# Two-layer audio trunk on one core: the tokens around the inner norms in two halves, squares summed on TensorE

## The reference

```
for layer in range(DEPTH):
    h = rms_norm(x, norm_mix_pre[layer])
    if layer % 2 == 0:
        m = even_mixer(h, w_in, ..., w_out)      # RG-LRU branch and stick-breaking attention
    else:
        m = odd_mixer(h, positions, w_qkv, sinks, w_o)   # sliding-window attention with rotary
    x = x + rms_norm(m, norm_mix_post[layer])
    h = rms_norm(x, norm_ffn_pre[layer])
    f = conv_ffn(h, w_up, conv_w, conv_b, w_down)        # D_FF = 2816, gated, width-3 conv
    x = x + rms_norm(f, norm_ffn_post[layer])
```

## Time and profile before

| | |
|---|---|
| time, median of 3 runs | 1190.69 us (1187.4 to 1191.2) |
| the profiled execution: its own time | 1188.73 us |
| its span | 1186.9 us |
| PE busy | 1149.5 us (97% of the span), 5888 matmuls |
| DVE busy | 692.9 us (58%) |
| ACT busy | 486.1 us (41%) |
| POOL busy | 73.2 us (6%) |
| TensorE clock granted, mean | 0.993 |

### The profile page before, as it was taken

The page is one execution under the profiler, slowest core; times in us unless marked ns, Lnnn a source line. Parts: engine busy times, 40 slices in busy tenths (PEclk is TensorE's granted clock), DMA queues, the critical chain, the costliest instruction groups (busy, mean ns, idle before and its releaser), DMA issues.

```text
span 1186.9 us, 14989 instructions
## 1 busy us (share of the span) xinstructions
PE 1149.5 (97%) x5888; PEld 959.4 (81%) x5888; DVE 692.9 (58%) x840; ACT 486.1 (41%) x667; POOL 73.2 (6%) x57
## 2 busy tenths in 40 slices
PE   8999999999999999999999998899999999999997
PEld 6875777777888888888887788786888888899997
DVE  5745455558876766732228677248877766752222
ACT  4555655434533443431123229334444443433220
POOL 3000000122000000000112100033000000000000
PEclk9999999999999999999999999999999999999999
DMA  6312112222333332322321541041423333332221
GB/s 212 107 36 72 36 36 71 71 72 71 107 84 93 106 104 77 103 98 98 98 98 36 156 129 49 1 126 34 135 79 105 106 88 88 106 98 65 96 99 71
DMA packets 147477, 104.39 MB, mean 88 GB/s; under 512 B 4642, under 2 KB 144354, under 8 KB 147426
## 3 DMA queue, kind: packets, MB, share of 16 engines
q1 hardware_dynamic: 146466, 102.36, 29.0%
q10 hardware_dynamic: 960, 1.31, 0.5%
HBM read 98.02 MB, written 2.10 MB: 84 GB/s over the span
## 4 chain that ended last, share of the span: by engine, by line
PE 84%; DVE 7%; ACT 6%; issue 1%; POOL 0%; DMA 0%; POOLq 0%; SPq 0%; DVEq 0%; ACTq 0%
PE ps L1283 25%; PE ps L1285 25%; PE ps L1284 25%; DVE x L1076 3%; PE ps L1480 2%; PE ps L1468 2%; ACT hx_hi L656 1%; DVE hx_lo L1080 1%; ACT prob L772 1%; PE ps L1491 1%; PE ps L1352 1%; ACT w_hi L522 1%; PE ps L1345 1%; PE ps L1504 1%; PE ps L1660 1%
## 5 line engine op out<-in xcount | busy, mean ns | idle before, releaser
L1283 PE MATMUL ps<-hx_hi,w_hi 128*128 128x512 f32 x912 | 360.5, 395 | 2.7 <-DVE hx_lo L1080 2.5
L1284 PE MATMUL ps<-hx_lo,w_hi 128*128 128x512 f32 x912 | 355.9, 390 | 0.0
L1285 PE MATMUL ps<-hx_hi,w_lo 128*128 128x512 f32 x912 | 355.7, 390 | 0.0
L810 DVE TENSOR_TENSOR w_lo<-w_raw,w_hi 128x2048 fp32r<-128x2048 f32 (+1 forms) x90 | 201.9, 2243 | 169.5 <-ACT w_hi L522 169.4
L522 ACT ACTIVATE w_hi<-w_raw 128x2048 fp32r<-128x2048 f32 (+1 forms) x90 | 168.4, 1871 | 159.2 <-DMA w_raw<-in_ffn_w_down 113.8
L1283 PEld LDWEIGHTS ps<-hx_hi,w_hi 128*128 128x128 f32 x912 | 171.5, 188 | 45.8 <-DVE hx_lo L1080 7.2
L1285 PEld LDWEIGHTS ps<-hx_hi,w_lo 128*128 128x128 f32 x912 | 171.6, 188 | 36.3
L1284 PEld LDWEIGHTS ps<-hx_lo,w_hi 128*128 128x128 f32 x912 | 171.7, 188 | 35.2 <-issue 0.7
L1283 PE MATMUL ps<-w_hi,g_hi 128*128 128x256 f32 x352 | 99.2, 282 | 0.0
L1285 PE MATMUL ps<-w_hi,g_lo 128*128 128x256 f32 x352 | 98.9, 281 | 0.0
L1284 PE MATMUL ps<-w_lo,g_hi 128*128 128x256 f32 x352 | 98.9, 281 | 0.0
(11 more groups left out here) (202 smaller groups left out, 1524.1 us busy)
## 6 DMA issues: line engine op xcount, KB each, us to landing
w_raw<-in_ffn_w_up SPq DMA_DIRECT2D x88, 512.0 KB, 5.0
w_raw<-in_ffn_w_down SPq DMA_DIRECT2D x16, 1024.0 KB, 5.1
w_raw<-in_even_w_in SPq DMA_DIRECT2D x8, 1024.0 KB, 5.1
w_raw<-in_ffn_w_down SPq DMA_DIRECT2D x8, 768.0 KB, 4.4
w_raw<-in_odd_w_qkv SPq DMA_DIRECT2D x6, 1024.0 KB, 5.0
w_raw<-in_even_w_out SPq DMA_DIRECT2D x4, 1024.0 KB, 5.1
w_raw<-in_odd_w_o SPq DMA_DIRECT2D x4, 1024.0 KB, 5.7
x_in<-in_x SPq DMA_DIRECT2D x4, 512.0 KB, 6.4
```

The lines of the kernel that those rows point to most:

```text
L810: dve.tensor_tensor(w_lo[s][:, 0:k], w_raw[s][:, 0:k], w_hi[s][:, 0:k], ALU.subtract).then_inc(w_lo_done, 1)
L1283: pe.matmul(dst, s_hi, r_hi, start=first, stop=False)
L1284: pe.matmul(dst, s_hi, r_lo, start=False, stop=False)
L1285: return pe.matmul(dst, s_lo, r_hi, start=False, stop=last)
```

## The change

- **Halves.** At each boundary the last units of the first product (units 1, 2 and 3 of an output projection; the last three of the down projection) are computed for tokens 0 to 255 first, all of them, and then for tokens 256 to 511. The first two units of the next product are done the same way. A matmul there has 256 columns instead of 512, and there are twice as many. The two output tiles of a half share a bank.
- **The first norm** is done per half: `post_mean_square` and `post_spread` for half 0 stand inside half 1 of the first product, those for half 1 inside half 0 of the next product. POOL still adds most squares of m; the last square buffer goes into PE's sum directly (6 one-column matmuls per half).
- **The second norm's squares** aren't added on POOL: PE multiplies each of the eight squared tiles with the column of ones (`mean_square(p, i)`, 4 one-column matmuls each), and there are three buffers `sq`, freed by PE.
- `keep_clock` is no longer called at the boundaries.
- **Copies** of m out of PSUM for the halved units are made by ACT; DVE keeps m·g·r in PSUM (columns 256 to 511 of bank 6 or 7) instead of in `m`.
- **Extra slots.** The first unit of each up projection has a weight slot of its own. Its load needs no ring slot, only that the attention of its layer is over.
- **Small moves.** `split_at` splits unit u+4 at the first unit of an up projection and nothing at the second and third. Layer 0's unit 2 of the output projection is no longer used as filling before `ya_ready`. `sw_values` (layer 1's attention) takes its eight products in the order 0, 4, 1, 5, 2, 6, 3, 7; the first four write partitions 0 to 63, the others 64 to 127.

```diff
 def split_at(layer, u):
-    return {0: u + 3, 1: u + 3, 2: None}.get(u - U_UP[layer], u + 2)
+    return {0: u + 4, 1: None, 2: None}.get(u - U_UP[layer], u + 2)
...
 # ACT
-    for i in range(DT):
-        act.wait_ge(x_new, DT * bi + i + 1)
-        act.activation(hx_hi[:, i, :], x[:, i, :], ACT.Identity, scale=gain(which, layer, i)).then_inc(hx_hi_done, 1)
-        square(n + 1, i, x[:, i, :])
-    split_hi(u + 2)
-    root(n + 1)
+    act.preload_act_table_set("sqrt_and_others")
+    for j, v in enumerate(last):
+        half_out(bi, 0, j, v)          # square, and copy to m
+    post_root(bi, 0)
+    if bi != 1:
+        half_out(bi, 1, 0, last[0])
+    for i in range(DT):
+        hi(0, i)
+        if i == (4 if bi == 1 else 3):
+            split_hi(splits[0])
+        if i == 5 and bi != 1:
+            half_out(bi, 1, 1, last[1])
+    half_out(bi, 1, len(last) - 1, last[-1])
+    split_hi(splits[1])
+    post_root(bi, 1)
+    for i in range(DT):
+        hi(1, i)
+        square(bi + 1, i, x[:, i, :])  # from i = 3 on: waits for PE's sum of square i - 3
+        if i == (3 if bi == 1 else 5):
+            split_hi(splits[2])
+    root(bi + 1)
...
 # PE
-def mean_square(n):
-    ...
+def mean_square(p, i):
+    if i == 0:
+        pe.wait_ge(pstd_done, 2 * p)
+    pe.wait_ge(sq_done, DT * p + i + 1)
+    for t in range(TT):
+        last = pe.matmul(bank(6)[:, t:t + 1], sq[i % 3][:, P * t:P * t + P], ones[:, 0:1], start=i == 0 and t == 0,
+                         stop=i == DT - 1 and t == TT - 1, skip_group_check=True)
+    last.then_inc(xms_mm, 1)
...
-    mean_square(n)
-    keep_clock(7, 6)
-    spread(n)
-    keep_clock(13, 7)
-    first_two(u, ...)
-    spread(n + 1)
+def first_units(bi, u):
+    pe.wait_ge(ahalf_evac, a_copied)
+    for j in range(2):
+        unit_ready(u + j)
+        for k in range(UK):
+            if j == 0 and k == 3:
+                post_mean_square(bi, 1)
+            if j == 0 and k == 6:
+                post_spread(bi, 1)
+            pe.wait_ge(hx_ready, DT + 2 * DT * bi + k + 1)
+            first_half(u + j, 0, k)
+    pe.wait_ge(group_evac, evac)
+    for k in range(UK):
+        pe.wait_ge(hx_ready, 2 * DT + 2 * DT * bi + k + 1)
+        for j in range(2):
+            last = first_half(u + j, 1, k)
+            ...
+        if k >= 2:
+            mean_square(bi + 1, k - 2)
+    unit(u + 2, hx, hooks={(0, 0): lambda: mean_square(bi + 1, DT - 2), (0, 1): lambda: mean_square(bi + 1, DT - 1),
+                           (0, 5): lambda: spread(bi + 1)})
...
+ # out_halves(layer), h = 0 then 1, units 1 to 3, 8 tiles each:
+                    for k in ks[j]:
+                        if h and step == 3:
+                            ...
+                            post_mean_square(bi, 0)
+                        if h and step == 5:
+                            post_spread(bi, 0)
...
-            for e in range(8):
+            for e in (0, 4, 1, 5, 2, 6, 3, 7):
```

More of the change, by code:

```diff
@@ L54 @@
 G_SHIFT = N_DOWN - 4
[L57 to L63, removed]
+HALF = T // 2
+N_BOUNDARY = 3
 V_CONV = 64
@@ L375, in load_cols @@
             slot_free(u)
-            load(u, cols(w, c0), whole(u % RING))
+            load(u, cols(w, c0), whole(slot(u)))
         w_in, w_qkv = io["even_w_in"][0], io["odd_w_qkv"][0]
@@ L461, in load_up @@
                 for b in range(2):
-                    load(u, cols(w_up, j * P + F * b, P), w_raw[u % RING][:, :, b, :])
-            for j in range(2):
+                    load(u, cols(w_up, j * P + F * b, P), w_raw[slot(u)][:, :, b, :])
+            if layer == 0:
+                sp_.wait_ge(av_mm, SB_HEADS)
+            else:
+                sp_.wait_ge(o_mm, NCH)
+            for j in range(4):
                 load_up(U_UP[layer] + j, j)
@@ new lines, in boundary, with hi @@
+        def boundary(bi, which, layer, last, splits):
+            def hi(h, i):
+                act.wait_ge(x_new, 2 * DT * bi + DT * h + i + 1)
+                act.activation(hx_hi[:, i, tokens_of(h)], x[:, i, tokens_of(h)], ACT.Identity,
+                               scale=gain(which, layer, i)).then_inc(hx_hi_done, 1)
+            act.preload_act_table_set("sqrt_and_others")
[19 more added lines that the diff above has]
+            root(bi + 1)
@@ L1516, in out_part, with out_half, down_half, first_half @@
                 last.then_inc(unit_done, 1)
+        def out_half(layer, j, h, k, first, last):
+            u = U_OUT[layer] + j
+            hi, lo = mixer_out(layer, k)
+            for b in range(2):
+                dst = bank(group_banks(group_of(u)) + h)[:, tokens_of(b)]
+                ins = three(dst, *weights(u, k, b), hi[:, tokens_of(h)], lo[:, tokens_of(h)], first and b == 0, last and b == 1)
+            return ins
+        def down_half(u, h, k, k0):
+            for b in range(2):
+                dst = bank(group_banks(group_of(u)) + h)[:, tokens_of(b)]
+                ins = three(dst, *weights(u, k - k0, b), g_hi[:, k, tokens_of(h)], g_lo[:, k, tokens_of(h)],
+                            k == 0 and b == 0, k == FT - 1 and b == 1)
+            return ins
+        def first_half(u, h, k):
+            for b in range(2):
+                dst = bank(group_banks(group_of(u)) + h)[:, tokens_of(b)]
+                ins = three(dst, *weights(u, k, b), hx_hi[:, k, tokens_of(h)], hx_lo[:, k, tokens_of(h)], k == 0 and b == 0,
+                            k == UK - 1 and b == 1)
+            return ins
         pe.wait_ge(consts_cast, 1)
@@ L1552, in _ @@
[L1552 to L1570 removed]
+        out_whole(0, [7], end=True)
@@ L1572, in ffn @@
+        def out_projection(layer):
+            if layer == 1:
+                pe.wait_ge(y_ready, NCH)
+                banks_free(group_of(U_OUT[1]))
+                unit_ready(U_OUT[1])
+                out_whole(1, range(UK), first=True, end=True)
+            out_halves(layer)
         def ffn(layer, bi):
             u0 = U_UP[layer]
-            n = 4 * layer + 1
-            boundary(n, bi, u0)
-            for j in range(2, 5):
+            first_units(bi, u0)
+            for j in range(3, 5):
@@ L1583, in ffn @@
             g_up = group_of(U_DOWN[layer])
-            for mp in range(4):
+            for mp in range(3 + layer):
                 b0 = group_banks(g_up + mp)
@@ L1618, in _ @@
         ffn(0, 0)
-        boundary(3, 1, U_QKV)
-        for k in range(2, N_QKV):
+        down_halves()
+        first_units(1, U_QKV)
+        for k in range(3, N_QKV):
             u = U_QKV + k
```

507 lines of the change are left out of this document (322 added, 185 removed).

## The result

| | before | after |
|---|---|---|
| median (range) | 1190.95 us (1187.4 to 1191.22, 4 executions) | 1206.89 us (1198.41 to 1210.45, 4 executions) |
| profiled execution, span | 1188.73, 1186.9 us | 1210.45, 1208.7 us |
| mean granted clock over the span | 0.993 | 0.975 |
| PE busy, matmuls | 1149.5 us, 5888 | 1172.8 us, 6734 |

The ratio is 1.0131, 95% interval [1.0074, 1.0187]: the kernel became 16 us slower. 1194.5 was forecast. The profiled execution of after is the slowest of its four (1210.45 us, mean clock 0.975); the fastest took 1198.41 us at 0.987.

What follows compares the result with a forecast made beforehand. PE's stream was taken as the bound: boundary work -1.8, waits +8.3 and attention -1.5 gave +5.0 us, 1193.7 from the profiled run or 1195.7 on the median's scale; 1194.5 was taken, range 1183 to 1203 (8 in 10).

Steps and rivals of the forecast that it cites:

- The stall for `hx_lo`: Second half of each boundary: PE waits for hx_lo behind ACT's weight split, 1.2 us three times, 3.6 us.
- `ya_lo`: Layer 0, before `ya_ready`: 18 matmuls no longer cover PE's wait for the recurrent branch, 1.2 us.
- the first QKV unit: Boundary 1: its weights are loaded and split at 18.6 us but wanted at 17.4, a wait of 1.2 us.
- the fifth QKV unit: After boundary 1: its weight split ends later than PE wants it, a wait of 0.7 us with the hand-over.
- The sixth up unit: Up projections: DVE's weight split comes about 0.8 us late, a wait of 1.6 us in both layers.
- Waits of the change together: PE's new waits at five places: 3.6 + 1.2 + 1.2 + 1.6 + 0.7 = 8.3 us.
- the term of -1.5 us: Layer 1's attention: the new product order saves 0.6 us per chunk, only the last three chunks counting; bounds 0 and -3.
- DVE's chain decides: Boundaries: DVE takes 2 us per tile, PE waits 3 to 4 us per boundary; +16 us, 1205; chance 0.1.
- -1.8 + 8.3 - 1.5: Whole kernel: PE's work at the boundaries, its new waits and the attention's product order, together +5.0 us.
- the fourth rival: Half 1 of each boundary: one clock fall costing 2 to 5 us; +13 us, 1202; chance 0.1.

Runs made afterwards that it cites:

- before_sw_order: The kernel before with only the order of the eight value products per chunk changed to 0, 4, 1, 5, 2, 6, 3, 7: 1190.38 us, ratio 1.000.
- split_late: The kernel after with the third weight split of each boundary moved behind the last tile: 1195.42 us, ratio 1.005.
- ones_stationary: The kernel after with one 512-column matmul per tile, ones stationary, instead of four one-column matmuls for the squares of x: 1181.24 us, ratio 0.991.
- filled: The kernel after with two 512-column dummy matmuls ahead of five of the eight groups of sums in each second half: 1206.72 us, ratio 1.013.
- half_passes: The kernel after with two of the four one-column matmuls per group left out for tiles 1 to 7: 1186.40 us, ratio 0.997.

## Why the prediction was wrong

**What held.** The steps on PE came out as written. A tile of the second half takes 2.30 us (2.36 reckoned), a group of sums 0.81, and the matmul behind it is 0.08 late: 0.89, where 0.94 was reckoned. 256-column matmuls start 0.118 to 0.120 apart. The stall for `hx_lo` came once per boundary: 3.4 us in all (3.6). `ya_lo` 1.0 (1.2); the first QKV unit 1.2 (1.2, the row with "issue"); the fifth QKV unit 1.5 (0.7). The sixth up unit was not waited for, where 1.6 was put; the second output unit was, 0.65, unforeseen. Waits of the change together: 7.8 us, 8.3 predicted. That this total is so close is in part luck: a wait of 1.6 that did not come is made up by 0.65 at a place not foreseen and 0.8 more at the fifth QKV unit. The order 0, 4, 1, 5 makes a chunk 0.92 us long (16 passes from 764.65 to 765.57) from start to start and 1.09 from first start to last end, where the earlier trace rows has 1.58, 0.5 less as reckoned (0.6), but by before_sw_order the attention gives little or nothing of it on: the term of -1.5 us is not shown.

```profile
764.65 1.09 PE L1933 MATMUL ps<-probT,v1s 128*64 128x128 f32 x16
765.57 1.04 PE L1933 MATMUL ps<-probT,v 128*64 128x128 f32 x16
```

**What is left without the clock.** The profiled executions differ by 1210.45 - 1188.73 = 21.7 us; 5.0 were forecast. They differ by 60 - 17 = 43 us at the lower clock, some 37 of them at the boundaries; at 0.45 us each, the price measured between after and split_late, that is 19 us, and +3 us remain. By the medians it is 15.9 us at mean clocks of 0.981 and 0.991, of which 1.0 us per 0.001 is 10: +6 remain. Split_late, with the falls at boundaries 0 and 2 gone and one of 7 us left at boundary 1, measured +4.2 us against the 1191.18 beside it. The sum of +5.0 was right to about 2 us.

**The rival with the right number.** "DVE's chain decides" gave +16 us, 1205, close to what was measured, but not for what happened. It asked for 256-wide DVE instructions near 0.7 us, 2 us a tile, and waits of 3 to 4 us a boundary. In after they take 0.42 (the add) and 0.48, a tile of half 0 takes DVE 1.25 us (262.77 to 264.02), and PE's waits for `hx_lo` are 3.4 us in all three boundaries.

**The step that failed** is the clock. The forecast's sum, -1.8 + 8.3 - 1.5, has no term for it, which puts it at nothing. It stood only in the fourth rival, "the clock falls in half 1", at +13 us and a chance of 0.1, against which was said "PE waits less than before". Two things were wrong there.
- *Its size.* It was priced by the fall before: 4 us long, 1.3 to 2 us lost, in a stretch of product matmuls of 512 columns. After has 16.4, 7.2 and 17.2 us at the lower clock and loses 7.6 at boundary 0 alone, four to six times the old fall's price and more than the 2 to 5 us a boundary that the rival allowed. The fall did not end with the wait: the last three matmuls of tile 6, all of tile 7, four groups of sums and fifteen 512-column matmuls of unit 2 ran at the lower clock (281.93 to 298.32).
- *Its chance.* The total of PE's waits at the boundaries hardly went down: 7.8 us after, against 8.8 before in these three rows (us in total, times, longest):

```profile
PE ps L1345 <- POOL sumsq L509: 5.7, 4, 1.4
PE ps L1283 <- DVE hx_lo L1080: 2.5, 12, 0.2
PE ps L1357 <- DVE diag L820: 0.6, 1, 0.6
```

And the total is not what mattered. The one wait for `hx_lo` in each boundary stands right behind a group of one-column passes, in a stretch that is a third such passes. The prediction had both facts, the wait's place and 40% of passes, in two different paragraphs and did not put them together.

A rule of the Trainium skill stood there as well: "TensorE: Matmul & The Clock Gate", section "What's actually happening", by which the clock follows how busy PE has been. Read by the busy time of the records it called this change safe. The trace does not agree with that reading: 25.36 of 26.50 us were recorded busy at a mean clock of 0.69, and 17.07 of 17.07 at 0.50.

**What stays open.** Which property of a one-column pass counts (its single column, or the loading of 128x128 of weights for each) was not tried apart; ones_stationary took away both. Why boundary 1 has two short falls in after where boundaries 0 and 2 have one of 17 us isn't explained either, nor what starts the falls that have no wait in front. All lengths at the lower clock are of one profiled execution per kernel; that after's four executions range from 1198.41 at a mean clock of 0.987 to 1210.45 at 0.975 shows that they vary, and that the time goes with them, 1.0 us per 0.001. At 0.987 some 31 us of the span are at the lower clock instead of 60, so the fastest execution cannot have had falls as long as the profiled one.

## What to carry to other kernels

A one-column float32 matmul used to sum over partitions costs 0.2 us of PE, nearly as much as a 512-column matmul of the product, and where such passes filled a third of a stretch, a wait of 1 us in it went with a loss of 8. So before moving a reduction onto a full PE, look for an engine that has the time: POOL had it here, and with it the rest of the same change gained 18 us instead of losing 16. When a forecast puts a wait somewhere, look at what surrounds it and give the clock a price of its own there.

## Unexpected of the hardware

- With all of its time recorded busy (17.07 of 17.07 us), PE stood at 1.2 GHz for 17 us on end.
- The clock also fell where PE had not waited for 8 to 14 us, right behind three groups of one-column passes (filled, boundary 0; after, boundary 1).
- A group of eight one-column passes took 0.81 us at the full clock and 1.57 at the lower one: it scales with the clock like a long matmul (0.12 and 0.21 us for 256 columns).
- Where one-column passes are left out, the clock can be worth more than the passes: 9.5 us of passes gave 20.5 us (half_passes).
